# Hybrid encoder step, Mamba-2 mixer: transposes of the old-state parts in a row, decays of the first group tile by tile, and a share of the work at the mixer's end moved from VectorE to GpSimd

## The chip, the cores and the metric

One NeuronCore of one Trainium2 chip runs the whole program in one launch. The metric is the device time of one execution in microseconds (us); for before it is the median of three runs. Engines are called PE (TensorE), DVE (VectorE), ACT (ScalarE), POOL (GpSimd) and SP (SyncE, which issues the loads of the weights).

## The reference

One inference step of a two-layer trunk for 384 tokens: 256 of a new stream and 16 each of 8 running streams. Layer 0 has a Mamba-2 mixer, layer 1 latent attention; each is framed by two half-step SwiGLU blocks. The change lies in the mixer of layer 0 and where it hands over to the SwiGLU block behind it. What that mixer computes, cut from the reference:

```python
z, xbc, dt_raw = split(u @ w_in)                 # u: RMSNorm of h, 384 x 1024
xbc = silu(causal_conv(xbc, conv_buf, conv_w, conv_b))
xs, Bm, Cm = split(xbc)                          # 32 heads of 64; 4 groups with a state of 128
dt = softplus(dt_raw + dt_bias); A = -exp(A_log)
# ssd_scan, chunk by chunk:
seg    = exp(where(causal, acs_l - acs_s, -inf)) # acs = cumsum(dt * A)
y_diag = einsum(C_l . B_s * seg, xs * dt)
y_off  = einsum(C_l, state) * exp(acs)
state  = state * exp(acs[-1]) + einsum(B, xs * dt * exp(acs[-1] - acs))
y = rmsnorm((y_diag + y_off + D * xs) * silu(z), norm_g)
h = h + y @ w_out
```

Then follows `h = h + 0.5 * swiglu(rmsnorm(h, ln_ffn2[0]), ...)`, whose first products need the new h.

## The kernel before, in words

**Layout.** Activations lie transposed, features on the 128 partitions and the 384 tokens along the free axis; TT = 3 token tiles of 128: tiles 0 and 1 are the new stream, tile 2 the samples. All weights come as one stream of blocks of 128 x 1024 fp32 into four slots (`raw`). ACT copies a block into its rounded part `whi` (`hi_split`), DVE subtracts to get `wlo` (`lo_split`), and PE computes each product of 128 columns as three matmuls, xh*whi, xl*whi and xh*wlo (lines 1786 to 1788); 24 of them use up one block. A slot is free for ACT when PE has counted the block in `blk`, and for SP's next load when its `lo_split` has counted `lo_ready`.

**Order.** Nothing is scheduled automatically: each engine has its own program, written by hand, and the semaphores tie them. Around the weight stream each engine walks the same list MIX_ORDER of blocks.

**The mixer** goes over GROUPS = 4 groups g. A group has ten input blocks in_proj(g, 0..9): 0 to 3 are x, 4 and 5 are B and C, all six with a convolution (three DVE steps, L1290) and a silu on ACT; 6 to 9 are the gate z. After block 6 stand `turns(g)` (PE transposes B and x, and multiplies B and C), after 7 `first_states`, after 8 `old_state`. `y_tile(g, t)` forms the output of tile t for the eight heads of the group, in PSUM banks 0 to 3: for t >= 1 first the old-state part `yoff`, brought in by a matmul against the identity (L1979), then per head the matmul of `seg` with `xdt` (L1983), both per bank in turn. It waits for `seg`: POOL loads the cumulative sums spread over rows, ACT makes differences (`seg_diff`, eight instructions a tile, L815) and exponentials (L820), DVE multiplies by the masked C.B (`decay_cb`, L1360). `sample_states(g, 0..3)` adds to the sample streams' states (L2002; DVE's `state_add`, L1388; POOL decays them before, L556).

**y.** DVE's `y_rows` (L1395 to L1401) adds D*xs, gates with z, and splits y into `yh` (ACT) and `yl`; ACT squares it, DVE sums the squares over all groups in `sqacc` (`y_square_sum`, L1430). out_proj(g, 0..3) multiplies y with four blocks, two output columns j each; DVE adds them to `facc` (L1412, L1414). Those of group g run among group g+1's input blocks.

**The mixer's end.** For the last group y lies in `xh` and `xl` at 4 to 7. PE multiplies ones with `sqacc` for the mean square (L2056), ACT takes the root, DVE the reciprocal (L1499), and `residual(b)` scales two columns of facc (L1419) and adds them to h (L1420). `x_hi` (ACT, L695) and `x_lo` (DVE, L1174) split the new h for the SwiGLU block `gate_up(1, 2)`, whose weight blocks are gu1, gu1+1, ... PE takes gu1 column by column as x_lo delivers (L1786), then gu1+1, then the matmul of the norm's sum of squares (L1802, `norm_sum`), which DVE sums from ACT's squares (L1517, L1520).

## Time and profile before

| | |
|---|---|
| median of 3 runs | 1923.78 us (1918.68 to 1928.84) |
| profiled execution | 1929.4 us, its span 1927.6 us |
| granted PE clock, mean | 0.981 |
| PE busy | 1858.5 us (96%) |
| DVE busy | 1143.1 us (59%) |
| ACT busy | 828.4 us (43%) |
| POOL busy | 226.5 us (12%) |

The profiled execution lies 5.6 us above the median. The times of the rows are from its span's start; the mixer runs from about 290 to 655 us, its groups some 79 us each. PE busy says that an instruction was there, not at which clock; the column PEclk does. A group of rows at one line can mix shapes.

### The profile page before, as it was taken

What the parts mean: (1) busy time and instruction counts of PE and PEld (TensorE: products, weight loads), DVE (VectorE), ACT (ScalarE), POOL (GpSimd) and SP (SyncE); (2) the same over time, 40 slices, a digit from 0 to 9 for tenths busy, and PEclk for the clock granted to TensorE, in tenths of its full rate; (3) what the DMA queues carried; (4) which work ended last, traced back from release to release, by engine and by line L of the source; (5) the groups of instructions that cost most, each with busy time, mean ns of one, the idle gap of its engine ahead of it and who ended that gap; (6) DMA issues with size and microseconds to landing.
All of it is one profiled execution on the core that took longest, in us unless ns stands there. A gap on an engine that the chain in (4) does not pass through costs nothing.

```text
span 1927.6 us, 28305 instructions
## 1 busy us (share of the span) xinstructions
PE 1858.5 (96%) x10584; PEld 1758.3 (91%) x10584; DVE 1143.1 (59%) x1733; ACT 828.4 (43%) x1427; POOL 226.5 (12%) x283
## 2 busy tenths in 40 slices
PE   9999998999999899999999999998998999999997
PEld 8999998698888899999999999986777889999997
DVE  6455448587787845544674454445777745554444
ACT  5333226463564433323453333336666534333333
POOL 1000111203202000002310001113102131000110
PEclk9999999799999999999999999999999999999999
DMA  5444444354452444444444444441124533444441
GB/s 201 131 127 123 142 133 151 95 208 157 166 202 70 164 131 125 123 139 137 121 123 126 131 130 133 134 147 58 45 66 125 178 113 116 122 121 129 143 132 65
DMA packets 67652, 249.71 MB, mean 130 GB/s; under 512 B 8328, under 2 KB 9608, under 8 KB 66288
## 3 DMA queue, kind: packets, MB, share of 16 engines
q1 hardware_dynamic: 57584, 205.32, 34.8%
q0 software_dynamic: 9984, 43.24, 6.6%
q8 instruction: 56, 0.92, 0.2%
q14 instruction: 28, 0.23, 0.0%
HBM read 235.74 MB, written 12.12 MB: 129 GB/s over the span
## 4 chain that ended last, share of the span: by engine, by line
PE 85%; DVE 8%; ACT 3%; issue 1%; DMA 1%; POOL 0%; SPq 0%; DVEq 0%; ACTq 0%; POOLq 0%
PE pair L1786 23%; PE pair L1787 23%; PE pair L1788 23%; PE pair L2202 2%; PE pair L2203 1%; PE pair L2204 1%; DVE wlo L1164 1%; PE pair L1983 1%; PE pair L1793 1%; PE pair L1795 1%; PE pair L1794 1%; PE pair L2002 1%; ACT seg L815 1%; PE pair L2284 1%; PE pair L1979 1%
## 5 line engine op out<-in xcount | busy, mean ns | idle before, releaser
L1786 PE MATMUL pair<-xh,whi 128*128 128x384 f32 x1960 | 665.3, 339 | 14.8 <-DVE xl L1174 12.6
L1788 PE MATMUL pair<-xh,wlo 128*128 128x384 f32 x1960 | 658.6, 336 | 0.0
L1787 PE MATMUL pair<-xl,whi 128*128 128x384 f32 x1960 | 658.5, 336 | 0.0
L1164 DVE TENSOR_TENSOR wlo<-raw,whi 128x1024 fp32r<-128x1024 f32 (+3 forms) x372 | 463.2, 1246 | 180.5 <-ACT whi L686 171.7
L686 ACT ACTIVATE whi<-raw 128x1024 fp32r<-128x1024 f32 (+2 forms) x369 | 378.9, 1029 | 296.2 <-PE pair L1788 283.0
L1786 PEld LDWEIGHTS pair<-xh,whi 128*128 128x128 f32 x1960 | 371.1, 189 | 26.1 <-issue 15.0
L1787 PEld LDWEIGHTS pair<-xl,whi 128*128 128x128 f32 x1960 | 371.2, 189 | 1.8 <-issue 1.2
L1788 PEld LDWEIGHTS pair<-xh,wlo 128*128 128x128 f32 x1960 | 370.7, 189 | 0.0
L1184 DVE TENSOR_TENSOR tg<-pair,rstd 128x384 f32<-128x384 f32 x88 | 49.0, 557 | 332.5 <-PE pair L1788 331.8
L1786 PE MATMUL pair<-ah,whi 128*128 128x384 f32 x704 | 237.0, 337 | 3.5 <-DVE tu L1185 3.3
L1787 PE MATMUL pair<-al,whi 128*128 128x384 f32 x704 | 236.5, 336 | 0.0
L1788 PE MATMUL pair<-ah,wlo 128*128 128x384 f32 x704 | 236.5, 336 | 0.0
L705 ACT ACTIVATE tg<-tg 128x384 f32<-128x384 f32 x88 | 46.4, 527 | 350.0 <-DVE tu L1185 350.0
L1786 PEld LDWEIGHTS pair<-ah,whi 128*128 128x128 f32 x704 | 132.3, 188 | 4.7 <-DVE tu L1185 4.7
L1787 PEld LDWEIGHTS pair<-al,whi 128*128 128x128 f32 x704 | 132.4, 188 | 0.0
L1788 PEld LDWEIGHTS pair<-ah,wlo 128*128 128x128 f32 x704 | 132.3, 188 | 0.0
L527 POOL TENSOR_TENSOR sqacc<-h 128x384 f32<-128x384 f32 x6 | 5.8, 974 | 816.4 <-DVE h L1212 762.7
L695 ACT ACTIVATE xh<-h,gains 128x384 fp32r<-128x384 f32 x64 | 37.0, 612 | 119.1 <-DVE h L1212 102.6
L529 POOL TENSOR_TENSOR sqt<-h 128x384 f32<-128x384 f32 x42 | 36.6, 872 | 288.9 <-DVE h L1212 266.4
L1657 DVE TENSOR_REDUCE sqacc<-kn 128x8 f32<-128x512 f32 x64 | 43.5, 681 | 25.3 <-ACT kn L1024 25.0
L530 POOL TENSOR_TENSOR sqacc<-sqacc,sqt 128x384 f32<-128x384 f32 x42 | 58.0, 1381 | 3.3
L709 ACT ACTIVATE ah<-tu 128x384 f32 (+1 forms) x88 | 46.4, 527 | 22.6 <-DVE tu L1188 22.6
(393 smaller groups left out, 2252.5 us busy)
## 6 DMA issues: line engine op xcount, KB each, us to landing
raw<-in_stream SPq DMA_DIRECT2D x372, 512.0 KB, 3.6
S<-in_ssm POOLq DMA_DIRECT2D x4, 2048.0 KB, 8.7
out_ssm_s<-S POOLq DMA_DIRECT2D x4, 2048.0 KB, 8.0
seg<-acs_rows POOLq DMA_DIRECT2D x12, 512.0 KB, 4.9
cTb<-in_cacheT POOLq DMA_DIRECT2D x10, 512.0 KB, 4.0
kn<-rs_rows SPq DMA_DIRECT2D x16, 264.0 KB
lowC<-in_cache SPq DMA_DIRECT2D x8, 512.0 KB, 3.2
lowA<-in_cacheT POOLq DMA_DIRECT2D x6, 512.0 KB, 5.2
```

The lines of the kernel that those rows point to most:

```text
L530: step(pool.tensor_tensor(acc, acc, sqt[:, :], ALU.add))
L686: A(whi[:, r, 0:w], raw[:, r, 0:w], ACT.Copy).then_inc(hi_ready, 1)
L695: A(xh[:, k, :], h[:, k, :], ACT.Copy, scale=gains[:, m, k:k + 1]).then_inc(xh_ready, 1)
L705: A(tg[:, j, :], tg[:, j, :], ACT.Silu).then_inc(sg_ready, 1)
L709: A(ah[:, i * 2 + (n0 // 2 + j), :], tu[:, j, :], ACT.Copy).then_inc(ah_ready, 1)
L1164: V.tensor_tensor(wlo[:, r, 0:w], raw[:, r, 0:w], whi[:, r, 0:w].bitcast(F32), ALU.subtract).then_inc(lo_ready, 1)
L1184: V.tensor_tensor(tg[:, j, :], bank[2 * j][:, 0:TOK], r, ALU.mult)
L1657: V.reduce_sum(ksq[:, st, b, 8 * g:8 * g + 8], kn[:, w % 2, 0:512].rearrange("p (h d) -> p h d", h=8), axis=AX.X).then_inc(past_sum, 1)
L1786: M(out, whi[:, r, ws], mh_(k), start=first and k == k0, stop=False)
L1787: M(out, whi[:, r, ws], ml_(k), start=False, stop=False)
L1788: ins = M(out, wlo[:, r, ws], mh_(k), start=False, stop=last and k == k1 - 1)
L2202: M(bank[w % 2][:, :], ch, wkh[:, k, half], start=k == 0, stop=False)
```

## The change

It touches five things.

1. **Old-state parts.** In `y_tile`, for t >= 1, the four parts of `yoff` are brought into banks 0 to 3 by four transposes in a row, ahead of all eight heads, instead of one fp32 matmul against the identity per bank.
2. **Group 0.** ACT's silu of block 5 comes before `decay_exps`; `seg_diff` and the exponential alternate tile by tile, tiles 0 and 1 behind block 8, tile 2 behind block 9. DVE's `decay_cb(0, t)` and PE's `y_tile(0, 0)` stand where the other groups have them.
3. **Group 3.** ACT's `seg_diff(3, 2)` comes behind block 6's silu.
4. **Sums of squares** of y go from DVE to POOL in all groups, after the store of the states; DVE's gate evacuations wait for POOL's count (`sq_step`).
5. **The end.** y of group 3 has tiles of its own (`yh3`, `yl3`, in the space of `xdt` and `seg`), so all of xh and xl is free for the new h. PE's mean square comes ahead of out_proj(3, 0), and `sample_states(3, 3)` behind it. DVE evacuates two columns in one instruction (`f_add`). POOL splits the blocks gu1, gu1+1 and gu1+2, and for the last two columns scales the sum of groups 0 to 2 and adds it to h, while DVE adds the last group's part straight from PSUM. DVE takes up its own splits when POOL's last one has counted; `state_add(3, 2)` moves behind that.

PE, group 1, the second token tile, before (`pair` are the PSUM banks, L1979 the old-state part, L1983 the heads):

```order
L1979 MATMUL pair<-ident,yoff 128x128
L1983 MATMUL pair<-seg,xdt 64x128 x2
L1979 MATMUL pair<-ident,yoff 128x128
L1983 MATMUL pair<-seg,xdt 64x128 x2
L1979 MATMUL pair<-ident,yoff 128x128
L1983 MATMUL pair<-seg,xdt 64x128 x2
L1979 MATMUL pair<-ident,yoff 128x128
L1983 MATMUL pair<-seg,xdt 64x128 x2
```

and now, with the states of the first two streams and the third tile behind it (the same lines are L2007, L2011 and L2030 there):

```order
L2007 MATMUL pair<-ident,yoff 128x128 x4
L2011 MATMUL pair<-seg,xdt 64x128 x8
L2030 MATMUL pair<-xw,Bm 128x512 x2
L2007 MATMUL pair<-ident,yoff 128x128 x4
L2011 MATMUL pair<-seg,xdt 64x128 x8
```

The kinds no longer alternate within a tile; nothing else moved between them.

ACT, group 0, from the end of in_proj(0, 7) to the gates, before (whi is a block's split, seg the decays, zs the gates):

```order
L686 ACTIVATE whi<-raw 128x1024 [waits blk,raw_loaded0]
L815 ACTIVATE seg<-seg,acs 128x128 [waits seg_ld0]
L815 ACTIVATE seg<-seg,acs 128x128 x7
L815 ACTIVATE seg<-seg,acs 128x128 [waits seg_ld1,act_chain]
L815 ACTIVATE seg<-seg,acs 128x128 x7
L815 ACTIVATE seg<-seg,acs 128x128 [waits seg_ld2,act_chain]
L815 ACTIVATE seg<-seg,acs 128x128 x7
L820 ACT_TABLE_LOAD
L820 ACTIVATE seg<-seg 128x1024 [waits act_chain]
L820 ACTIVATE seg<-seg 128x1024 x2
```

and now:

```order
L721 ACTIVATE whi<-raw 128x1024 [waits blk,raw_loaded0]
L850 ACTIVATE seg<-seg,acs 128x128 [waits seg_ld0]
L850 ACTIVATE seg<-seg,acs 128x128 x7
L854 ACTIVATE seg<-seg 128x1024 [waits act_chain]
L850 ACTIVATE seg<-seg,acs 128x128 [waits seg_ld1]
L850 ACTIVATE seg<-seg,acs 128x128 x7
L854 ACTIVATE seg<-seg 128x1024 [waits act_chain]
L721 ACTIVATE whi<-raw 128x1024 [waits blk,raw_loaded1]
L850 ACTIVATE seg<-seg,acs 128x128 [waits seg_ld2]
L850 ACTIVATE seg<-seg,acs 128x128 x7
L854 ACTIVATE seg<-seg 128x1024 [waits act_chain]
```

Each tile's exponential follows its differences, and no table load stands between them.

DVE at the mixer's end, from the last two residuals to the norm's sums, now (L1455 is f_add, L1471 and L1472 the residual, L1220 x_lo, L1210 a split, L1432 state_add, L1544 and L1547 the sums of squares):

```order
L1455 TENSOR_TENSOR facc<-facc,pair 128x768 [waits blk]
L1471 TENSOR_TENSOR facc<-facc,rstd 128x768 [waits f_evac]
L1472 TENSOR_TENSOR h<-h,facc 128x768 [waits dve_chain]
L1220 SCALAR_TENSOR_TENSOR xl<-h,gains,xh 128x384 [waits xh_ready] x2
L1471 TENSOR_TENSOR facc<-pair,rstd 128x768 [waits h_part,blk]
L1472 TENSOR_TENSOR h<-h,facc 128x768 [waits dve_chain]
L1220 SCALAR_TENSOR_TENSOR xl<-h,gains,xh 128x384 [waits xh_ready] x2
L1210 TENSOR_TENSOR wlo<-raw,whi 128x1024 [waits hi_ready,lo_ready]
L1432 TENSOR_TENSOR S<-S,pair 128x512 [waits s_dec,state_ps]
L1432 TENSOR_TENSOR S<-S,pair 128x512 [waits s_dec]
L1544 TENSOR_TENSOR sqacc<-facc 128x384 [waits sq_step]
L1547 TENSOR_TENSOR sqacc<-sqacc,facc 128x384 [waits sq_step,dve_chain] x6
```

and beside it POOL, which had nothing there before but the store:

```order
L554 TENSOR_TENSOR sqacc<-sqacc,zs 128x384 [waits y_sq]
L554 TENSOR_TENSOR sqacc<-sqacc,zs 128x384 [waits y_sq,sq_step] x3
L561 TENSOR_TENSOR wlo<-raw,whi 128x1024 [waits lo_ready,hi_ready,sq_step]
L591 TENSOR_TENSOR facc<-facc,rstd 128x768 [waits f_evac,y_rstd]
L594 TENSOR_TENSOR h<-h,facc 128x768 [waits h_part]
L561 TENSOR_TENSOR wlo<-raw,whi 128x1024 [waits lo_ready,hi_ready] x2
L598 DMA out_ssm_s<-S 128x4096 [waits state_ready]
```

Three splits, a scaling and an add left DVE's row for POOL's, and DVE's split of gu1+3 waits for `lo_ready`.

The diff, cut to its core:

```diff
@@ tiles
+            with ExitStack() as rows_first:
+                xdt = sb("xdt", [P, TT, 512], F32, rows_first)
+                seg = sb("seg", [P, TT, 1024], F32, rows_first)
+            yh3 = sb("yh3", [P, 4, TOK], F32R, ssd)
+            yl3 = sb("yl3", [P, 8, TOK], F32R, ssd)
@@ helpers
         def y_hi(g, k):
-            return yh[:, k, :] if g < GROUPS - 1 else xh[:, 4 + k, :]
+            return (yh if g < GROUPS - 1 else yh3)[:, k, :]
+        def y_summed(g):
+            return 3 * KD - 2 + 4 * (g + 1)
@@ GpSimd
+            def y_square_sum(g):
+                for i in range(4):
+                    pool.wait_ge(y_sq, 4 * g + i + 1)
+                    if g or i > 1:
+                        step(pool.tensor_tensor(sqacc[:, 0, :], sqacc[:, 0, :], zs[:, i, :], ALU.add))
+                    elif i == 1:
+                        step(pool.tensor_tensor(sqacc[:, 0, :], zs[:, 0, :], zs[:, 1, :], ALU.add))
+
+            def lo_split(n):
+                pool.wait_ge(hi_ready, n + 1)
+                pool.wait_ge(lo_ready, n)
+                pool.tensor_tensor(wlo[:, n % SLOTS, :], raw[:, n % SLOTS, :], whi[:, n % SLOTS, :].bitcast(F32),
+                                   ALU.subtract).then_inc(lo_ready, 1)
...
+                if g == GROUPS - 1:
+                    y_square_sum(g)
+                    lo_split(BASE["gu1"])
+                    pool.wait_ge(y_rstd, 1)
+                    pool.wait_ge(f_evac, 8 * g)
+                    pool.tensor_tensor(facc[:, 6:8, :], facc[:, 6:8, :], bc(rstd[:, 0, :], (P, 2, TOK), 1),
+                                       ALU.mult).then_inc(h_part, 1)
+                    pool.wait_ge(h_part, 1)
+                    pool.tensor_tensor(h[:, 6:8, :], h[:, 6:8, :], facc[:, 6:8, :], ALU.add).then_inc(h_part, 1)
+                    lo_split(BASE["gu1"] + 1)
+                    lo_split(BASE["gu1"] + 2)
                 pool.wait_ge(state_ready, 8 * g + 8)
                 pool.dma_start(T["ssm_s"][g], S[:, :, :]).then_inc(s_store, 16)
                 if g < GROUPS - 1:
+                    y_square_sum(g)
                     pool.wait_ge(s_store, 16 * (g + 1))
                     pool.dma_start(S[:, :, :], T["ssm"][g + 1]).then_inc(s_ld, 16)
@@ ScalarE
                 in_proj(g, 5)
                 if g == 0:
+                    silu(0, 5)
                     decay_exps()
-                else:
+                elif not last:
                     seg_diff(g, 2)
...
                 in_proj(g, 6)
+                if last:
+                    seg_diff(g, 2)
...
                 in_proj(g, 8)
                 if g == 0:
-                    for t in range(TT):
+                    for t in range(2):
                         seg_diff(g, t)
-                    seg_exps(g)
+                        seg_exp(g, t)
                 in_proj(g, 9)
+                if g == 0:
+                    seg_diff(g, 2)
+                    seg_exp(g, 2)
...
+            hi_split(n + 3)
+            for b in range(3):
+                x_hi(2, 2 * b)
+                x_hi(2, 2 * b + 1)
+                hi_split(n + 4 + b)
+            for k in range(4):
+                x_square(k)
+            x_hi(2, 6)
+            x_hi(2, 7)
             for k in range(4, KD):
                 x_square(k)
@@ VectorE
                     if g:
-                        dve.wait_ge(y_sq, 4 * g)
+                        dve.wait_ge(sq_step, y_summed(g - 1))
...
             def residual(b):
                 two = slice(2 * b, 2 * b + 2)
-                dve.wait_ge(f_evac, 8 * (GROUPS - 1) + 2 * b + 2)
-                step(V.tensor_tensor(facc[:, two, :], facc[:, two, :], bc(rstd[:, 0, :], (P, 2, TOK), 1), ALU.mult))
+                if b < 3:
+                    f_add(GROUPS - 1, b)
+                    dve.wait_ge(f_evac, 8 * (GROUPS - 1) + 2 * b + 2)
+                    src = facc[:, two, :]
+                else:
+                    dve.wait_ge(blk, CRED + out_block(GROUPS - 1, b) + 1)
+                    dve.wait_ge(h_part, 2)
+                    src = f_pair(GROUPS - 1, b)
+                step(V.tensor_tensor(facc[:, two, :], src, bc(rstd[:, 0, :], (P, 2, TOK), 1), ALU.mult))
                 V.tensor_tensor(h[:, two, :], h[:, two, :], facc[:, two, :], ALU.add).then_inc(h_new, 2)
...
+            n = out_block(GROUPS - 1, 0)
+            f_add(GROUPS - 2, 2)
+            lo_split(n + 1)
+            f_add(GROUPS - 2, 3)
+            lo_split(n + 2)
             dve.wait_ge(y_std, 1)
-            step(V.reciprocal(rstd[:, 0, :], std[:, :]))
+            V.reciprocal(rstd[:, 0, :], std[:, :]).then_inc(y_rstd, 1)
+            lo_split(n + 3)
+            dve.wait_ge(y_rstd, 1)
+            for b in range(4):
+                residual(b)
+                x_lo(2, 2 * b)
+                x_lo(2, 2 * b + 1)
...
+            dve.wait_ge(lo_ready, BASE["gu1"] + 3)
             gate_up(1, 2, norm_square_sum)
@@ TensorE
+                if t:
+                    for i in range(4):
+                        nc.tensor.transpose(bank[i][:, tiles(t)], yoff[:, t - 1, tiles(i)], ident[:, :])
                 for i in range(4):
-                    if t:
-                        M(bank[i][:, tiles(t)], yoff[:, t - 1, tiles(i)], ident[:, :], start=True, stop=False,
-                          skip_group_check=True)
...
             out_proj(GROUPS - 2, 3)
+            pe.wait_ge(sq_step, y_summed(GROUPS - 1))
+            M(bank[5][:, 0:TOK], ones[:, :], sqacc[:, 0, :], start=True, stop=True).then_inc(y_sum_ps, 1)
             out_proj(GROUPS - 1, 0)
-            pe.wait_ge(state_ready, 8 * GROUPS - 2)
-            pe.wait_ge(y_sq, 4 * GROUPS + 1)
-            M(bank[4][:, 0:TOK], ones[:, :], sqacc[:, 0, :], start=True, stop=True).then_inc(y_sum_ps, 1)
+            pe.wait_ge(y_std, 1)
+            sample_states(GROUPS - 1, 3)
```

## Rows read from the trace of the kernel before

**Rows 1.** Page: busy time and share of the span; then the chain's shares.
```profile
PE 1858.5 (96%) x10584; PEld 1758.3 (91%) x10584; DVE 1143.1 (59%) x1733; ACT 828.4 (43%) x1427; POOL 226.5 (12%) x283
...
PE 85%; DVE 8%; ACT 3%; issue 1%; DMA 1%; POOL 0%; SPq 0%; DVEq 0%; ACTq 0%; POOLq 0%
```

**Rows 2.** Windows: stretch, its us, busy us per engine, PEclk, DMA share, GB/s.
```profile
358.11:377.90 19.79, 19.79 (x82) 12.03 (x83) 6.39 (x9) 1.12 (x3) 2.66 (x3) 0.50 0.31 105
440.80:458.80 18.00, 18.00 (x121) 13.74 (x120) 13.20 (x18) 4.79 (x8) 7.24 (x7) 1.00 0.53 162
573.90:578.70 4.80, 0.15 (x1) 0.00 (x0) 3.32 (x6) 4.75 (x16) 0.00 (x0) 0.73 0.40 109
578.70:583.00 4.30, 4.26 (x21) 4.26 (x21) 3.56 (x7) 4.29 (x5) 0.00 (x0) 0.51 0.40 122
```

**Rows 3.** PE timeline: start, us, line, operation, count, [idle before, its releaser].
```profile
334.26 1.49 PE L1945 MATMUL pair<-BC 128*128 128x128 f32 x6
...
358.11 1.98 PE L1983 MATMUL pair<-seg,xdt 128*64 128x128 f32 x16 [3.13 <-DVE seg L1360]
...
380.73 1.13 PE L2002 MATMUL pair<-xw,Bm 32*128 32x512 f32 x4
...
440.83 1.09 PE L1983 MATMUL pair<-seg,xdt 128*64 128x128 f32 x16
446.16 0.38 PE L1979 MATMUL pair<-ident,yoff 128*128 128x128 f32 x2
...
449.20 1.13 PE L2002 MATMUL pair<-xw,Bm 32*128 32x512 f32 x4
...
458.85 1.13 PE L2002 MATMUL pair<-xw,Bm 32*128 32x512 f32 x4
...
505.44 1.47 PE L1949 MATMUL pair<-ident,xsT 128*128 128x128 f32 x12
...
578.74 0.90 PE L1937 MATMUL pair<-ident,BC 128*128 128x128 f32 x3 [4.69 <-ACT BC L771]
...
610.03 1.14 PE L2002 MATMUL pair<-xw,Bm 32*128 32x512 f32 x8
...
655.37 0.91 PE L1802 MATMUL pair<-sqacc,ones 128*128 128x384 f32 x2 [0.45 <-DVE sqacc L1520]
```

**Rows 4.** ACT timeline, group 0: differences, then exponentials of the decays.
```profile
343.04 7.41 ACT L815 ACTIVATE seg<-seg,acs 128x128 f32<-128x128 f32 x24
...
351.76 2.96 ACT L820 ACTIVATE seg<-seg 128x1024 f32<-128x1024 f32 x3
```

**Rows 5.** DVE timeline, group 0 and the mixer's end.
```profile
350.44 1.64 DVE L1164 TENSOR_TENSOR wlo<-raw,whi 128x1024 fp32r<-128x1024 f32 x1
...
356.84 3.49 DVE L1360 TENSOR_TENSOR seg<-seg,Gm 128x1024 f32<-128x1024 f32 x3
...
626.62 2.54 DVE L1499 RECIPROCAL rstd<-std 128x384 f32<-128x384 f32 x1
629.20 0.96 DVE L1419 TENSOR_TENSOR facc<-facc,rstd 128x768 f32<-128x768 f32 x1
...
632.28 1.01 DVE L1414 TENSOR_TENSOR facc<-facc,pair 128x384 f32<-128x384 f32 x2
...
651.79 3.52 DVE L1520 TENSOR_TENSOR sqacc<-sqacc,facc 128x384 f32<-128x384 f32 x6
```

**Rows 6.** Groups by line: count, busy us, mean ns, idle before; last a DMA issue.
```profile
L1164 DVE TENSOR_TENSOR wlo<-raw,whi 128x1024 fp32r<-128x1024 f32 (+3 forms) x372 | 463.2, 1246 | 180.5 <-ACT whi L686 171.7
...
L530 POOL TENSOR_TENSOR sqacc<-sqacc,sqt 128x384 f32<-128x384 f32 x42 | 58.0, 1381 | 3.3
L556 POOL TENSOR_TENSOR S<-S,dec 128x512 f32<-128x512 f32 x32 | 41.0, 1310 | 101.2 <-PE pair L1960 101.2
...
L568 POOL DMA_DIRECT2D S<-in_ssm x3 | 1.7, 557 | 23.2 <-DMA out_ssm_s<-S 23.2
...
seg<-acs_rows POOLq DMA_DIRECT2D x12, 512.0 KB, 4.9
```

More of the change, by code:

```diff
@@ L787, in in_proj @@
                       ACT.Copy).then_inc(cout_ready, 1)
[L788 removed]
+                if 1 <= b <= 6 and (g or b < 6):
                     silu(g, b - 1)
@@ L1485, in _ @@
                 if g == 0:
-                    for t in range(TT):
-                        decay_cb(g, t)
+                    decay_cb(g, 2)
                 state_add(g, 0)
```

143 lines of the change are left out of this document (49 added, 94 removed).

## The prediction

> **What bounds the kernel now.** I read the page first: TensorE (PE) is busy 96% of the span and holds 85% of the chain that ended last; VectorE (DVE) holds 8%, ScalarE (ACT) 3% [rows 1]. So a change of order pays only where PE waits, where its clock is low, or where its own work gets shorter. Next I read the windows of granted clock inside the mixer, 260 to 655 us. In group 0 there is a stretch of 19.8 us in which PE is busy throughout at a granted clock of 0.50, 1.2 instead of 2.4 GHz; it follows a wait. The same tiles of group 1 run at 1.00. In group 3 a wait of 4.7 us, with ACT busy through it, is followed by 4.3 us at 0.51 [rows 2]. The PE timeline then gives the waits and the price of each step [rows 3], and those of ACT, DVE and the POOL rows what the moved work costs [rows 4 to 6]. The reader should see in them that DVE, not PE, carries the mixer's end: from the last y matmul (610.03) to the norm matmul (655.37) are 45.3 us, and the norm matmul waits for DVE's sums.
>
> **The old-state parts.** In y_tile(g, 1) and (g, 2) PE now alternates a two-pass fp32 matmul (0.38 us) and a pair of 64-wide ones; a tile takes 449.20 - 446.16 = 3.04 us. Afterwards four transposes stand in a row, then eight heads. Twelve transposes in a row took 1.47 us, less the tail 0.11 each, so four take 0.44; eight heads in a row (16 passes) start 440.83 and cost about 1.02 before the next block [rows 3]. That is 1.46, so 1.6 us less per tile. There are two such tiles per group. PE is the bound there in groups 1 and 2, and DVE's y_rows waits for the last tile in group 3, so all six tiles of groups 1 to 3 count: **-9.5 us**. The two of group 0 give another 3.2 at full clock.
>
> **Group 0.** The wait is 3.13 us, ended by DVE's decay product L1360 [rows 3]. DVE has three such products in 3.49 us, behind evacuation 9 in its order [rows 5], and ACT first does all 24 differences (7.41 us) and then three exponentials (2.96) [rows 4]. After the change ACT does 8 differences (2.47) and one exponential (0.99). It starts when in_proj(0, 7) ends, near 341.5, and the exp table is still loaded, since silu no longer comes between. The first exponential ends near 345, DVE's product near 346.5. PE wants it after old_state(0), near 349. So this wait goes, with 2.5 us to spare. What is late next is tile 2: its product stands behind evacuation 9 and costs PE about 0.4. The clock: from the first tile to the end of in_proj(1, 0) group 0 takes 380.73 - 358.11 = 22.6 us; group 1 takes 458.85 - 440.83 = 18.0 for the same and one in_proj more (4.3 us, from the end of its first tile, 441.85, to 446.16), 13.7. The low clock costs 8.9 [rows 3]. A second edit: ACT's silu of block 5 no longer waits behind the decay exponentials and a table load, so the B transposes start at once; but the products of B and C still wait for those exponentials (they read its PSUM banks), and these begin 2.2 us later than before. I put the products at 333.0 instead of 334.26: 1.3 gained. The seg loads start 2.2 us later too, near 335.5; with 4.9 us to landing [rows 6] the first is there long before ACT's difference at 341.5, and the next have 3 and 7 us more. Sum: 3.1 + 8.9 + 3.2 + 1.3 - 0.4 = **-16.1 us**.
>
> **Sums of squares of groups 0 to 2.** DVE loses up to four adds of 384 per group. POOL gets them at 1.38 each [rows 6], 5.5 us. They stand there behind the store of the old states and ahead of the load of the next ones, and POOL already idles there for that store's landing, 23.2 us in three groups, 7.7 each [rows 6]: the adds fit in. Even if they didn't, that load runs in a stretch where PE needs the states only at the next first_states, some 30 us on. Evacuations 6 to 9 now wait for POOL's sum, done some 25 us earlier. I count nothing in groups 1 and 2. Two columns in one instruction free a PSUM bank 0.5 us later, about what the lighter DVE gives back.
>
> **Group 3.** PE waits 4.69 us for silu of B and C on ACT [rows 3], and ACT is busy for 4.75 of these 4.80 us [rows 2]. One difference tile, 2.47 us [rows 4], now stands behind that silu; of what DVE saves with its four adds (3.52 us for six such adds [rows 5], so some 2.4 for four) only about 0.3 arrives, because ACT is full. So 2.7 of 4.69 go and 2.0 stay. At 0.51 the 4.3 us behind it cost about 2.1. Whether the clock still falls after a wait of 2 us, the rows leave open, and I keep that cost: **-2.7**.
>
> **The mixer's end**, from the last y matmul as 0. y_rows on DVE is unchanged, 7.0 us. Then come two f_adds with two splits between; the second f_add waits for PE (out_proj(2, 3) ends at 9.4) and the reciprocal (2.54) ends at 14.5, where before it ended at 19.1. Before it PE needs POOL's four adds, 4.5 to 10.2, and waits for them some 0.9; PE has slack here. After one more split (15.6) come the residuals: f_add 1.0, product 0.96, add 0.96, ACT's hop 0.7, two x_lo about 1.1 (as two f_adds of 384, 1.01) [rows 5], with semaphores 4.8 us each, the last without its f_add 3.8: 33.8 if nothing disturbs them. But POOL works from 20.7: a split, a product and an add of 768, two splits. An add of 384 takes 1.38 and a product of 512 takes 1.31 us [rows 6]; by length the split of 1024 lies between 2.6 and 3.7. I take 3.6 and 2.8 for 768, since both inputs are whole tiles as in the 384 add; together 16.4, to 37.6 with the hops. h_part arrives at 30.2, before residual(3) wants it at 32. Next to POOL a DVE split took 1.64 instead of 1.25 us [rows 5, 6]; I add a third to DVE's SBUF-only work, 1.0 per residual, three times: 36.9. ACT then has the last squares and the split of gu1+3, to 38.5; DVE's own split 1.2, a state_add 1.25 that came later before, and seven sums 4.1 (3.52 for six) [rows 5]: the norm matmul at 45.1 against 45.3. **About 0.** The three splits and two partial steps that leave DVE are given back by the wait for POOL's last split, the slower shared stretch and the state_add moved ahead of the sums.
>
> The Trainium skill (GPSIMD Engine Reference, Performance versus the Vector engine) measures tensor_tensor on GpSimd at 4497 ns for 2048 fp32 and about 2.6 cycles per element. That would make a split some 2.5 us, an estimate from that page; the end would stay, since DVE sets it.
>
> **Sum.** 9.5 + 16.1 + 2.7 + 0 = 28.3 us; I round the hand-made hops up to 28.8. The profiled execution took 1929.4 (span 1927.6) and would take 1900.6. It lies 5.6 above the median of the three runs, 1923.8, so the forecast for the median is **1895 us**, 1.5% faster.
>
> **Rivals.**
> - *DVE and POOL exclude each other at the end.* For it: the 1.64 us split. Against it: a full exclusion by POOL's 1.3 us products would give 2 us and more. Its price: POOL's 16.4 us and DVE's SBUF-only 9 us in a row from 20.4 end at 45.8 instead of 36.9, so 9 us are lost: 1904. The Trainium skill (SBUF — State Buffer, Who interferes with whom) states it so: a DVE instruction with two SBUF inputs and a GpSimd instruction that reads SBUF use one pair, whoever comes first keeps it for its whole instruction. The rows show a third more, not that. 10%.
> - *The clock in group 0 stays low* because the tiles are light work, not because of the wait. Against it: group 1's tiles run at 1.00 [rows 2]. Price: 8.9 less what shorter tiles save, about 7: 1902. 7%.
> - *Transposes in a row don't cost 0.11* ahead of 64-wide matmuls (0.42 each, 1.2 us per tile, eight tiles): 10 us lost, 1905. 5%.
> - *The end gains too* (no disturbance, clock kept in group 3): 2 to 8 us more, 1887 to 1893; the main case reaches down to 1889. 12%.
> - *Slower:* POOL's splits starve PE. gu1, gu1+1 and gu1+2 can't be multiplied before POOL has split them, and DVE itself waits for the last. Five POOL operations stand in that chain; the gain of 28.8 is eaten when they take 45 instead of 16.4 us, 9 us each. The price at 11 us each is 38 us: 1933. For it: nothing in the trace shows a 1024-long POOL operation. Against it: by length 3.7 at most, and twice that loses 16 of 28.8. 2%.
> - *The change only swaps waits*, within 0.5%: group 0's first product is late again because seg lands late (its exponential would have to be 7 us later). Then 3.1 and 8.9 us stay lost and 16.8 are gained, 1907; with the end 9 us worse as well, 1916. 4%, the half of it within 0.5%.
>
> **Chances and range.** Main case 1895 (1889 to 1901): 60%. The rivals as given. The 8-in-10 range takes in the lock, the clock and the transposes: 1885 to 1905. A measurement of this kernel tells about 0.5% (9.6 us) from no change; only the last two cases and a part of the bad ends together reach above 1914: faster 0.94, same 0.04, slower 0.02.
>
> **What would show it.** No PE wait on the decay product before the first y tile and a clock near 1.00 from there on; y tiles 1 and 2 in 1.5 us; PE's wait in turns(3) near 2 us; POOL's splits near 3.6 us with no PE wait on them; DVE split and residual products a third longer beside them; the norm matmul 45 us behind the last y matmul. Wrong at once: a y tile still at 3 us, a clock of 0.50 in group 0, or a POOL split over 5 us.

## The result, and the profile after

Against the kernel before the change, run beside it, the ratio is 0.9905, 95% interval 0.9888 to 0.9923: medians 1907.42 us (six runs, 1901.71 to 1909.52) and 1924.02 (six runs, 1918.68 to 1928.84). It is faster by 0.95%, and the forecast of 1895 (1885 to 1905) was too good by 12 us. The profiled execution took 1907.38 us, span 1905.6, where the one of before took 1929.4, span 1927.6. The page after, busy times and the shares of the chain that ended last, against [rows 1]:

```profile
PE 1838.9 (97%) x10552; PEld 1747.1 (92%) x10552; DVE 1142.5 (60%) x1698; ACT 825.9 (43%) x1425; POOL 260.6 (14%) x303
...
PE 83%; DVE 9%; ACT 3%; issue 2%; DMA 1%; POOL 0%; SPq 0%; DVEq 0%; ACTq 0%; POOLq 0%
```

DVE's busy time hardly moved although work left it, and its share of the chain rose. The windows after (the columns of [rows 2]) are PE's products of B and C in group 0, the y tiles of group 0 with what stands between them, the like stretch of group 1, and the 4.7 us behind PE's wait in turns(3):

```profile
332.00:337.00 5.00, 4.49 (x20) 4.52 (x21) 3.59 (x7) 2.25 (x5) 2.75 (x4) 0.50 0.30 66
...
350.48:365.92 15.44, 15.04 (x114) 12.32 (x113) 12.95 (x18) 8.05 (x17) 6.98 (x7) 1.00 0.62 188
426.81:441.91 15.10, 15.10 (x115) 12.45 (x116) 13.33 (x18) 4.76 (x8) 7.22 (x7) 1.00 0.64 191
556.30:561.00 4.70, 4.67 (x25) 4.67 (x26) 4.45 (x9) 4.67 (x11) 0.00 (x0) 0.64 0.47 149
```

The tiles of group 0 ran at 0.50 in [rows 2] and run at 1.00 now; a short stretch ahead of them is at 0.50. PE's timeline after, the rows that answer to [rows 3]:

```profile
332.51 1.62 PE L1973 MATMUL pair<-BC 128*128 128x128 f32 x6 [2.03 <-ACT dec L844]
...
350.48 1.09 PE L2011 MATMUL pair<-seg,xdt 128*64 128x128 f32 x16
...
358.88 0.66 PE L2007 MATMUL pair<-ident,yoff 128*128 128x128 f32 x4 [0.40 <-DVE seg L1404]
...
365.92 1.13 PE L2030 MATMUL pair<-xw,Bm 32*128 32x512 f32 x4
...
381.47 0.41 PE L1814 MATMUL pair<-yh,whi 128*128 128x384 f32 x1 [0.44 <-DVE facc L1453]
...
426.81 1.09 PE L2011 MATMUL pair<-seg,xdt 128*64 128x128 f32 x16
...
434.75 0.66 PE L2007 MATMUL pair<-ident,yoff 128*128 128x128 f32 x4
435.34 1.09 PE L2011 MATMUL pair<-seg,xdt 128*64 128x128 f32 x16
436.36 1.13 PE L2030 MATMUL pair<-xw,Bm 32*128 32x512 f32 x4
...
556.33 0.55 PE L1965 MATMUL pair<-ident,BC 128*128 128x128 f32 x3 [2.08 <-ACT BC L806]
...
584.18 1.13 PE L2030 MATMUL pair<-xw,Bm 32*128 32x512 f32 x4
...
633.88 0.91 PE L1830 MATMUL pair<-sqacc,ones 128*128 128x384 f32 x2 [1.81 <-DVE sqacc L1547]
```

Read against [rows 3]: the first y tile starts 7.6 us earlier and waits for nothing; the end of group 0's tiles (365.92 against 380.73) has gained 14.8 us, the last y matmul (584.18 against 610.03) 25.85. Then the gain shrinks: from there to the norm matmul it took 45.3 us and takes 49.7. Behind the norm matmul both kernels take the same, 1272.2 and 1271.7. So of the terms that the forecast added up, the mixer's end missed most. There DVE's timeline shows

```profile
590.09 1.90 DVE L1445 SCALAR_TENSOR_TENSOR yl<-zs,ang,yh 128x384 fp32r<-128x384 f32 x2
...
592.78 1.49 DVE L1210 TENSOR_TENSOR wlo<-raw,whi 128x1024 fp32r<-128x1024 f32 x1
...
606.76 2.09 DVE L1471 TENSOR_TENSOR facc<-facc,rstd 128x768 f32<-128x768 f32 x1
608.96 2.44 DVE L1472 TENSOR_TENSOR h<-h,facc 128x768 f32<-128x768 f32 x1
612.09 1.98 DVE L1220 SCALAR_TENSOR_TENSOR xl<-h,gains,xh 128x384 fp32r<-128x384 f32 x2 [0.69 <-ACT xh L730]
613.99 0.94 DVE L1455 TENSOR_TENSOR facc<-facc,pair 128x768 f32<-128x768 f32 x1
614.96 2.15 DVE L1471 TENSOR_TENSOR facc<-facc,rstd 128x768 f32<-128x768 f32 x1
617.21 0.96 DVE L1472 TENSOR_TENSOR h<-h,facc 128x768 f32<-128x768 f32 x1
...
620.97 2.55 DVE L1472 TENSOR_TENSOR h<-h,facc 128x768 f32<-128x768 f32 x1
...
627.38 1.22 DVE L1210 TENSOR_TENSOR wlo<-raw,whi 128x1024 fp32r<-128x1024 f32 x1 [2.03 <-ACT whi L721]
```

and POOL's, the same stretch:

```profile
588.73 2.31 POOL L554 TENSOR_TENSOR sqacc<-sqacc,zs 128x384 f32<-128x384 f32 x2 [10.88 <-ACT zs L866]
592.16 2.96 POOL L554 TENSOR_TENSOR sqacc<-sqacc,zs 128x384 f32<-128x384 f32 x2 [1.12 <-ACT zs L866]
605.63 2.41 POOL L561 TENSOR_TENSOR wlo<-raw,whi 128x1024 fp32r<-128x1024 f32 x1 [10.51 <-ACT whi L721]
608.00 2.59 POOL L591 TENSOR_TENSOR facc<-facc,rstd 128x768 f32<-128x768 f32 x1
610.67 2.45 POOL L594 TENSOR_TENSOR h<-h,facc 128x768 f32<-128x768 f32 x1
613.59 2.71 POOL L561 TENSOR_TENSOR wlo<-raw,whi 128x1024 fp32r<-128x1024 f32 x1 [0.47 <-ACT whi L721]
620.36 2.36 POOL L561 TENSOR_TENSOR wlo<-raw,whi 128x1024 fp32r<-128x1024 f32 x1 [4.06 <-ACT whi L721]
```

Lay the two over each other. POOL's split ends at 605.63 + 2.41 = 608.04, DVE's product at 606.76 + 2.09 = 608.85, 0.81 later. POOL's product ends at 610.59, DVE's add at 611.40, 0.81 later; 616.30 and 617.11; 622.72 and 623.52. Four times DVE's instruction ends 0.80 to 0.81 us behind POOL's, however early it began: it stood still until POOL had done, and only then did its work. (It ends 0.81 behind and not 0.96, the length of its row alone; no row explains the 0.15.) The x_lo pair at 612.09 stands still as well, until POOL's add ends at 613.12. It works the other way round too: POOL's product begins at 608.00, while DVE's still runs, and its add at 610.67, while DVE's add does, so POOL's 2.59 and 2.45 hold up to 0.85 and 0.73 us of standing still. The f_add at 613.99, one of whose inputs is PSUM, runs beside a POOL split in its usual 0.94. Against 0.96 and 1.15 alone, the five stretched rows lose 1.13 + 1.48 + 0.83 + 1.19 + 1.59 = 6.2 us. Beside POOL's four adds of the squares, at 588.73 to 595.12, DVE's rows are stretched too: y_rows ends 7.7 us after its start, at 591.99, where before it took 6.9, and the split at 592.78 takes 1.49 instead of 1.22. These adds stay on POOL in all the experiments on the end below.

### The profile page after: what moved, and what is told of

The parts are those of the page before. It is cut to its first block, busy times and chain, and to the rows that moved or that the text cites. A ratio compares the mean times of both kernels' runs of the same rounds, so it can differ in the third digit from the quotient of the medians.

```text
span 1905.6 us, 28242 instructions
## 1 busy us (share of the span) xinstructions
PE 1838.9 (97%) x10552; PEld 1747.1 (92%) x10552; DVE 1142.5 (60%) x1698; ACT 825.9 (43%) x1425; POOL 260.6 (14%) x303
## 4 chain that ended last, share of the span: by engine, by line
PE 83%; DVE 9%; ACT 3%; issue 2%; DMA 1%; POOL 0%; SPq 0%; DVEq 0%; ACTq 0%; POOLq 0%
PE pair L1814 23%; PE pair L1816 23%; PE pair L1815 23%; PE pair L2227 2%; PE pair L2228 1%; PE pair L2229 1%; DVE cy L1336 1%; DVE wlo L1210 1%; DMA lowA<-in_cacheT 1%; PE pair L1821 1%; PE pair L1823 1%; PE pair L1822 1%; PE pair L2309 1%; ACT seg L850 1%; PE pair L2011 1%
## 5 line engine op out<-in xcount | busy, mean ns | idle before, releaser
L1814 PE MATMUL pair<-xh,whi 128*128 128x384 f32 x1928 | 652.4, 338 | 16.0 <-DVE xl L1220 13.6
L1816 PE MATMUL pair<-xh,wlo 128*128 128x384 f32 x1928 | 646.7, 335 | 0.0
L1815 PE MATMUL pair<-xl,whi 128*128 128x384 f32 x1928 | 646.5, 335 | 0.0
L1210 DVE TENSOR_TENSOR wlo<-raw,whi 128x1024 fp32r<-128x1024 f32 (+2 forms) x369 | 461.3, 1252 | 185.1 <-ACT whi L721 176.3
L1814 PEld LDWEIGHTS pair<-xh,whi 128*128 128x128 f32 x1928 | 363.9, 189 | 26.1 <-issue 14.4
L1815 PEld LDWEIGHTS pair<-xl,whi 128*128 128x128 f32 x1928 | 363.9, 189 | 1.5 <-issue 1.0
L1816 PEld LDWEIGHTS pair<-xh,wlo 128*128 128x128 f32 x1928 | 363.7, 189 | 0.0
L1685 DVE TENSOR_REDUCE sqacc<-kn 128x8 f32<-128x512 f32 x64 | 43.5, 681 | 25.7 <-ACT kn L1070 25.5
L1220 DVE SCALAR_TENSOR_TENSOR xl<-h,gains,xh 128x384 fp32r<-128x384 f32 x64 | 41.9, 686 | 25.5 <-ACT xh L730 25.4
```

The costliest lines, as they stand in the source:

```text
L1210: V.tensor_tensor(wlo[:, r, 0:w], raw[:, r, 0:w], whi[:, r, 0:w].bitcast(F32), ALU.subtract).then_inc(lo_ready, 1)
L1220: V.scalar_tensor_tensor(out=xl[:, k, :], in0=h[:, k, :], scalar=gains[:, m, k:k + 1], in1=xh[:, k, :].bitcast(F32), op0=ALU.mult, op1=ALU ...
L1685: V.reduce_sum(ksq[:, st, b, 8 * g:8 * g + 8], kn[:, w % 2, 0:512].rearrange("p (h d) -> p h d", h=8), axis=AX.X).then_inc(past_sum, 1)
L1814: M(out, whi[:, r, ws], mh_(k), start=first and k == k0, stop=False)
L1815: M(out, whi[:, r, ws], ml_(k), start=False, stop=False)
L1816: ins = M(out, wlo[:, r, ws], mh_(k), start=False, stop=last and k == k1 - 1)
```

## The experiments

In the table, "y end" is the start of the row behind the last y matmul, "norm" the norm matmul, both from PE's timeline, and the way between them.

| kernel | y end | norm | way | median us | ratio to before |
|---|---|---|---|---|---|
| before | 610.03 | 655.37 | 45.3 | 1924.0 to 1927.9, five medians | 1 |
| after | 584.18 | 633.88 | 49.7 | 1907.4 | 0.9905 (0.9888 to 0.9923) |
| e1_rows | 591.97 | 637.30 | 45.3 | 1911.0 | 0.9924 (0.9903 to 0.9946) |
| e2_group0 | 597.45 | 642.77 | 45.3 | 1913.7 | 0.9947 (0.9926 to 0.9968) |
| e3_end_only | 609.09 | 658.81 | 49.7 | 1933.8 | 1.0042 (1.0024 to 1.0059) |
| e4_pool_left_out | 581.72 | 625.20 | 43.5 | 1901.8 | 0.9885 (0.9864 to 0.9906) |
| e5_splits_on_dve | 583.96 | 629.35 | 45.4 | 1903.9 | 0.9873 (0.9850 to 0.9897) |
| e6_part_on_dve | 581.85 | 630.83 | 49.0 | 1904.6 | 0.9884 (0.9860 to 0.9908) |
| e7_all_on_dve | 580.95 | 626.06 | 45.1 | 1899.6 | 0.9862 (0.9837 to 0.9888) |
| e8_woven | 584.69 | 628.16 | 43.5 | 1899.1 | 0.9847 (0.9826 to 0.9869) |
| e9_one_input | 581.92 | 625.99 | 44.1 | one run | |
| e10_split_beside_reciprocal | 579.93 | 623.44 | 43.5 | 1899.1 | 0.9866 (0.9844 to 0.9888) |
| e11_single_columns | 581.89 | 623.83 | 41.9 | 1899.0 | 0.9855 (0.9830 to 0.9880) |
| e12_before_again | 611.01 | 656.34 | 45.3 | 1928.2 | 1.0013 (0.9995 to 1.0032) |

**The parts apart.** e1 is the kernel before with the transposes in a row and nothing else:

```
+                if t:
+                    for i in range(4):
+                        nc.tensor.transpose(bank[i][:, tiles(t)], yoff[:, t - 1, tiles(i)], ident[:, :])
                 for i in range(4):
-                    if t:
-                        M(bank[i][:, tiles(t)], yoff[:, t - 1, tiles(i)], ident[:, :], start=True, stop=False,
-                          skip_group_check=True)
```

> Kernel before, with the old-state parts transposed in a row and nothing else. If a transpose ahead of the 64-wide matmuls costs 0.11 us, as the trace of the changed kernel says (a tile in 1.56 instead of 3.04 us), six tiles give 9 us at full clock and the two of group 0, which still run at 1.2 GHz here, about 2.5 us each: a span 13 to 14 us below before. If part of that is lost again because VectorE becomes the bound behind the tiles, less than 9.

Measured: 18.1 us at the y end, where 13 to 14 were expected. Groups 1 to 3, from the first y tile of group 1 to the y end, took 610.03 - 440.83 = 169.2 and take 159.7: 9.5. The rest is group 0, and PE's timeline of e1 shows why:

```profile
359.51 1.83 PE L1983 MATMUL pair<-seg,xdt 128*64 128x128 f32 x16 [3.13 <-DVE seg L1360]
361.28 1.12 PE L1979 MATMUL pair<-ident,yoff 128*128 128x128 f32 x4
...
364.77 0.66 PE L1979 MATMUL pair<-ident,yoff 128*128 128x128 f32 x4
```

The wait of 3.13 us is as before, and the clock falls as before, but four transposes take 1.12 us in tile 1 and 0.66 in tile 2, 3.5 us later: the low stretch ends within tile 1, where [rows 2] has it last 19.8 us. The three traces with the alternating tiles and that wait (before, e3, e12) all have the long one. Five of e1's six runs lie within 1 us of the traced one (1910.7 to 1911.5), so its trace shows e1's usual case; still it is one trace. As far as it goes, either part, the row of transposes or the earlier decays, wins back most of the low clock, and the two gains can't be added.

e2 is the kernel before with the new order of group 0 alone (silu of block 5 first, differences and exponentials tile by tile, products and y_tile(0, 0) where the other groups have them):

```
+                    silu(0, 5)
                     decay_exps()
...
-                    for t in range(TT):
+                    for t in range(2):
                         seg_diff(g, t)
-                    seg_exps(g)
+                        seg_exp(g, t)
```

> Kernel before, with the order of group 0 alone (silu of block 5 first, decays tile by tile, first y tile ahead of block 9). The forecast had 12.9 us here without the two tiles (3.1 the wait, 8.9 the clock, 1.3 the products of B and C, less 0.4). The trace of the changed kernel says 11.7, because the low clock behind turns(0) now reaches into in_proj(0, 7). Rival: the clock stays at 1.2 GHz in the light tiles when these still alternate, then 4 us or less.

It gains 440.83 - 428.62 = 12.2 us to the first y tile of group 1 and 12.6 at the y end. The window from 350.20 to 366.00, with the alternating tiles in it, ran at 1.00. That rules out the prediction's rival by which the clock is low because the tiles are light work: without the wait the same tiles keep it. e1's 18.1 and e2's 12.6 would make 30.7; the changed kernel has 25.85, with group 3's part as well. The difference is, as far as rows show it, the clock counted twice.

e3 is the changed kernel with the transposes, group 0 and group 3 as before, so that the sums of squares and the new end are left:

```
-                if t:
-                    for i in range(4):
-                        nc.tensor.transpose(bank[i][:, tiles(t)], yoff[:, t - 1, tiles(i)], ident[:, :])
...
-                    silu(0, 5)
...
-                    seg_diff(g, 2)
```

> Changed kernel with the first three parts undone: alternating old-state parts, the old order of group 0 and of group 3's last differences. What is left is the end with GpSimd's share, the sums of squares on GpSimd and the paired evacuations. The forecast had about 0 for this. If the end is worse by the 4.4 us that the traces show between the last y matmul and the norm matmul, the time is 2 to 4 us above before (the lighter VectorE gives 1 to 2 back in group 3); at 0 or below, the loss lies elsewhere.

The end, with the sums on POOL and the paired evacuations, makes the kernel slower, by 0.42% (0.24 to 0.59), and its way is 49.7 us, the same as after. The spans differ by 4.4, which is the way; the medians by 7.4, where 2 to 4 were expected. For the other 3 us no row was found.

**Is it POOL?** e4 is the changed kernel without POOL's five steps at the end. No other engine does them, so three low parts, and in two columns of h the share of groups 0 to 2, are missing:

```
-                    lo_split(BASE["gu1"])
...
-                    pool.tensor_tensor(h[:, 6:8, :], h[:, 6:8, :], facc[:, 6:8, :], ALU.add).then_inc(h_part, 1)
+                        pool.wait_ge(hi_ready, n + 1)
+                        pool.wait_ge(lo_ready, n)
+                        pool.sem_inc(lo_ready, 1)
```

> Changed kernel in which GpSimd only counts its five steps at the end and does not do them: the splits of gu1, gu1+1 and gu1+2 and the two steps on columns 6 and 7 are left out, so the result lacks them. Theory (VectorE's instructions with two SBUF inputs stand still while GpSimd reads): seven of them took 7 us more than alone, so the norm matmul comes 6 to 7 us sooner, 43 instead of 49.7 us behind the last y matmul, and the span is 6 to 7 us shorter than the changed kernel's. Rival (the new order of splits, states and sums and the wait for ScalarE's split of gu1+3 cost it): at most 1 to 2 us shorter.

The way is 43.5, 6.2 less, and the stretched rows had lost 6.2. Every product and add of 768 is back at 0.96. So the new order of the end is worth 45.3 - 43.5 = 1.8 us if POOL's steps cost nothing, and DVE standing still for them takes 6.2.

e5, e6 and e7 give the steps back to DVE, in parts and together. The three splits go behind the adds of the residuals:

```
             for b in range(4):
                 residual(b)
+                if b:
+                    lo_split(n + 3 + b)
                 x_lo(2, 2 * b)
```

and residual(3) is done like the others:

```
-                if b < 3:
-                    f_add(GROUPS - 1, b)
...
-                    dve.wait_ge(h_part, 2)
-                    src = f_pair(GROUPS - 1, b)
+                f_add(GROUPS - 1, b)
```

> The changed kernel with its three splits of gu1 to gu1+2 back on VectorE, each between the add of a residual and its x_lo pair; GpSimd keeps the sums of squares and the product and add of residual(3). The way from the last y matmul to the norm matmul took 45.3 us before, 49.7 after and 43.4 with none of the five steps. Theory (each of the two engines stands still for the other's whole instruction): in the changed kernel the five steps stretch five VectorE instructions by 1.13, 1.48, 0.83, 1.19 and 1.59 us, 6.2 in all; here two steps are left, with some 2.5 of it, and the splits add 1.2 each less the 0.7 of the hop to ScalarE that each now fills: 43.4 + 2.5 + 1.5 = 47.4 us, 2.3 us under the changed kernel. Rival (the order of the end costs the time, not the other engine): VectorE gets 3.6 us of work more and wins nothing, 50 us or more.

> The changed kernel with residual(3) wholly on VectorE; GpSimd keeps the sums and the three splits. Theory: three stretched instructions, some 3.7 us, and on VectorE one f_add of 0.95 more, since product and add stood there already: 43.4 + 3.7 + 0.95 = 48.0 us from the last y matmul to the norm matmul, 1.7 under the changed kernel. Rival (order): VectorE has 0.95 more to do and the way is 50.6.

> The changed kernel with all five steps back on VectorE; GpSimd only sums the squares. Theory: no VectorE instruction is stretched; 43.4 + 0.95 + 1.5 = 45.9 us from the last y matmul to the norm matmul, 3.8 under the changed kernel, and a split and a product at 1.2 and 0.96 us throughout. Rival (order): 43.4 with less work, so at least 43.4 + 0.95 + 3.6 = 48, and with what the order costs the 49.7 of the changed kernel.

e7 has 45.1 where 45.9 was expected and the rival had 48 or more: with all five steps on DVE, three splits of 1.22 and an f_add of 0.95 more work, the way is 4.6 us shorter than after. e6, with POOL's three splits, has 49.0 (48.0 expected): in its DVE timeline the products next to them take 2.09, 2.68 and 2.63 us, 4.5 lost. e5 has 45.4 (47.4 expected): its two POOL steps cost 0.43 and 1.46 us, and DVE's splits cost less than I had put, since each fills the 0.7 us hop to ScalarE. The theory holds for all three; which steps are on POOL decides, not the order.

**Whose inputs matter?** e9 keeps POOL busy at the same places with steps that read less:

```
-                pool.tensor_tensor(wlo[:, n % SLOTS, :], raw[:, n % SLOTS, :], whi[:, n % SLOTS, :].bitcast(F32),
-                                   ALU.subtract).then_inc(lo_ready, 1)
+                pool.tensor_copy(wlo[:, n % SLOTS, :], raw[:, n % SLOTS, :]).then_inc(lo_ready, 1)
...
+                    pool.memset(facc[:, 6:8, :], 0.0).then_inc(h_part, 1)
...
+                    pool.memset(h[:, 6:8, :], 0.0).then_inc(h_part, 1)
```

> The changed kernel, but GpSimd's five steps at the mixer's end read less: the three splits are copies of raw (one SBUF input), the product and the add are constant fills (no input). It leaves out the low parts of three weight blocks and a quarter of the residual, so only the traces of the two engines are read. Theory (VectorE stands still only while a GpSimd instruction with two SBUF inputs runs, or one that reads SBUF at all): beside the fills no VectorE instruction is stretched, a product of 768 takes 0.96 us and an x_lo pair 1.15; beside the copies it decides which of the two it is. Rival (any GpSimd access to SBUF holds VectorE up, writes too): VectorE's products and adds beside the fills are stretched as in the changed kernel, to 2.0 us and more.

POOL's timeline of e9, and DVE's:

```profile
604.36 0.73 POOL L590 MEMSET facc<- 128x768 f32 x1
605.15 0.74 POOL L592 MEMSET h<- 128x768 f32 x1
608.69 1.04 POOL L561 CAST wlo<-raw 128x1024 fp32r<-128x1024 f32 x1 [2.80 <-ACT whi L719]
613.78 1.05 POOL L561 CAST wlo<-raw 128x1024 fp32r<-128x1024 f32 x1 [4.05 <-ACT whi L719]
```

```profile
604.50 0.96 DVE L1469 TENSOR_TENSOR facc<-facc,rstd 128x768 f32<-128x768 f32 x1
605.56 0.96 DVE L1470 TENSOR_TENSOR h<-h,facc 128x768 f32<-128x768 f32 x1
...
609.25 1.29 DVE L1469 TENSOR_TENSOR facc<-facc,rstd 128x768 f32<-128x768 f32 x1
...
614.41 1.22 DVE L1470 TENSOR_TENSOR h<-h,facc 128x768 f32<-128x768 f32 x1
```

Beside the two fills, which only write, DVE's product and add run in 0.96. Beside the copies, which read one tile, they are stretched, and end at 610.54 and 615.63, again 0.81 and 0.80 us behind POOL's 609.73 and 614.83. So both kinds of POOL read tried here, of two tiles and of one, hold up a DVE instruction with two SBUF inputs, and POOL's fills don't. The Trainium skill (SBUF — State Buffer, Who interferes with whom) states just that, with the pair kept for the whole instruction and DVE instructions of at most one SBUF input free of it; the runs agree in each point: the common 0.81 us behind POOL's end, and the f_add in its usual 0.94.

**A better end.** e8 is e7 with hops filled and the sums earlier:

```
             for b in range(3):
+                hi_split(n + 4 + b)
                 x_hi(2, 2 * b)
                 x_hi(2, 2 * b + 1)
-                hi_split(n + 4 + b)
...
-                if b:
-                    lo_split(n + 3 + b)
+                if b < 3:
+                    lo_split(n + 4 + b)
+                else:
+                    state_add(GROUPS - 1, 2)
```

> As the one before, with the order of the end woven anew: ScalarE splits a block high before each x_hi pair and the fourth gate_up block ahead of the last pair, VectorE has a split (behind the last residual the state_add) between every residual and its x_lo pair, and the norm's sums come ahead of the split of gu1+3. Theory: VectorE's work is the bound once it stands still for nobody; what fills its hops comes off: 43 to 43.5 us from the last y matmul to the norm matmul, some 6 us under the changed kernel, near 1900. Rival (PE is what paces the end): no gain against the kernel without weaving, 45.9.

43.5 us as expected, and 1899.1: faster than both kernels, with an interval wholly below that of the changed one. PE no longer waits for the sums. Against e7 the total gains nothing that can be told; e7's trace had reached the y end 3.7 us earlier.

e10 tests the same rule from the side where it allows something: one split on POOL, beside the reciprocal.

```
-            lo_split(n + 3)
+            dve.wait_ge(lo_ready, n + 4)
...
                     y_square_sum(g)
+                    lo_split(out_block(g, 3))
```

> The woven kernel, with one split given to GpSimd again, that of out_proj(3, 3), which falls beside VectorE's reciprocal (one SBUF input, 2.55 us). Theory (only VectorE instructions with two SBUF inputs stand still): the split runs 2.4 us beside the reciprocal and the f_add, the reciprocal stays at 2.55, and VectorE's way is up to 1.2 us shorter, less what is left of the split when the first product of the residuals wants to start: 42.5 to 43.2 us from the last y matmul to the norm matmul against 43.4. Rival (any two instructions exclude each other): the reciprocal stretches to 4 us or more and the way is 44.5 or more. The total moves by less than a measurement tells.

DVE's timeline of e10, then POOL's:

```profile
592.40 2.55 DVE L1523 RECIPROCAL rstd<-std 128x384 f32<-128x384 f32 x1 [0.39 <-ACT std L926]
596.14 0.95 DVE L1450 TENSOR_TENSOR facc<-facc,pair 128x768 f32<-128x768 f32 x1 [1.18 <-PE pair L1809]
```

```profile
593.45 2.40 POOL L561 TENSOR_TENSOR wlo<-raw,whi 128x1024 fp32r<-128x1024 f32 x1 [2.57 <-ACT whi L713]
```

The reciprocal, with its one SBUF input, takes its 2.55 us beside the split, and the split its 2.40, so the rule holds. The way stays 43.5: what DVE saves it waits for PE, 1.18 us in front of the first f_add.

e11 gives groups 0 to 2 their single-column evacuations back:

```
+                if g < GROUPS - 1:
+                    for x in range(2):
+                        j, src = 2 * b + x, f_pair(g, b)[:, x, :]
...
+                            V.tensor_tensor(facc[:, j, :], facc[:, j, :], src, ALU.add).then_inc(f_evac, 1)
```

> As the one before, and the f_adds of groups 0 to 2 free their PSUM columns one by one again instead of in pairs. In the changed kernel TensorE waits five times 0.44 us for such a pair in groups 1 to 3 (before: 0.36 and 0.95). Theory: those waits go or shrink, and from the first y tile of group 0 to the first of group 3 it takes about 1 us less than the changed kernel's 222.95 us. Rival (the pairs cost nothing, TensorE waits for VectorE's other work): as long as in the changed kernel. It would be the fastest of all, 1897 to 1899.

The five waits of 0.44 us are gone, and from the first y tile of group 0 to that of group 2 it takes 500.81 - 350.18 = 150.6 us against 152.2 after and in e7: 1.6 us. To group 3 the gain is 2.0 (221.0 against 222.95), and in the total it doesn't show.

**The spread.** e12 is the kernel before, unchanged.

> The kernel before, once more, for a second trace. Its runs lie in two groups, near 1921 and near 1929, with mean granted clocks of 0.985 to 0.987 and 0.980 to 0.981; the trace shown is of the upper group. Theory (the clock after a wait of TensorE comes back sooner in some runs): if this trace is of the lower group, every row agrees with the first trace but for one or two stretches behind a wait, where the granted clock is 0.50 in the one and near 1.00 in the other, and these hold the 5 to 8 us. Rival (the runs differ everywhere a little, by the DMAs): the distance to the first trace grows evenly. If it falls in the upper group, it agrees with the first trace within 1 us at the last y matmul (610.03) and tells nothing.

Its traced run (1930.5) fell in the upper group, agrees with the first trace within 1 us at the y end, and tells nothing of the lower one. What separates the two groups of before, 5 to 8 us, stays open. That a clock can differ at the same place is shown elsewhere. Behind PE's wait in turns(3), windows of after (above, 0.64) and of e4:

```profile
555.50:560.20 4.70, 4.69 (x35) 4.70 (x36) 4.60 (x9) 4.67 (x11) 0.00 (x0) 1.00 0.46 139
```

The waits are 2.08 and 2.06 us, the work is the same, and from there to the first y tile the changed kernel takes 573.43 - 556.33 = 17.1 us and e4 570.97 - 555.51 = 15.5. The changed kernel, e5, e8 and e11 have the long form, e4, e6, e7, e9 and e10 the short. At the end, behind a wait of 3.65 us for x_lo (e11, first) and of 3.66 (e10, second):

```profile
618.50:623.80 5.30, 5.30 (x30) 5.25 (x31) 5.09 (x9) 2.31 (x4) 0.00 (x0) 1.00 0.00 0
```

```profile
616.50:623.40 6.90, 6.86 (x30) 6.80 (x31) 6.66 (x11) 2.36 (x4) 0.00 (x0) 0.75 0.03 5
```

The same two blocks of matmuls take 5.3 us or 6.9; e8 has the long form too. That is the whole difference between e11's way and e10's, not an edit's doing.

## Why the prediction was wrong, step by step

- **Old-state parts, 9.5 us in groups 1 to 3: right, the last 0.4 by luck.** In e1 it is 9.5. Group 1's two tiles took 3.04 and 3.15 us (446.16 to 449.20, 450.26 to 453.41) and take 1.55 and 1.61 after (432.14 to 433.69, 434.75 to 436.36), which makes 3.03 per group and 9.1 in three groups. The other 0.4 is clock: from the wait in turns(3) to group 3's first y tile, before takes 17.5 us and e1 17.1.
- **Group 0, 16.1: 14.0.** The wait went, the clock held, tile 2 waits 0.40 for its product, all as forecast. The B and C products' 1.3 came to 0.25: they did start earlier (332.51), but behind that very wait of 2.03 the clock is 0.50 now (the window at 332), and first_states starts at 341.57 against 341.82. The step took an earlier start for a gain without asking what the clock does behind the wait that is left. How long it stays low differs from trace to trace of the same order: from these products to first_states it takes 9.1 us after and in e2, 6.2 in e4, e7, e9 and e10. Paired evacuations, which I had set at nothing, cost two waits of 0.44 before group 1's tiles where before had one of 0.36.
- **The share of the clock.** The 8.9 us that I gave to the vanished wait aren't that wait's alone: with transposes in a row the low stretch ended after some 3 us even with the wait (e1, one trace). That the sum still held is luck: the two were in one change. Added up from e1 and e2 it would have been at least 4.9 too high.
- **Group 3, 2.7: right.** The wait fell from 4.69 to 2.08. The low clock behind it stayed in some executions and not in others; I kept it at full price.
- **The end, "about 0": +4.4, the step that failed.** The overlap was wrong: DVE's instructions beside POOL were to run on, a third longer, 3 us in all. They stood still, and the five rows lost 6.2. The other 1.1 us is a start of the residuals 0.5 later and a wait of 0.55 for PE. In front of that later start stand the stretched y_rows, which I had "unchanged, 7.0 us", and the stretched split, and POOL's last add of squares, which was held up by DVE in turn. POOL was faster than sized (2.41 and 2.59 us against 3.6 and 2.8), which shortened the rows that stood still; by my sizes, an estimate, the loss would have been the rival's 9. That rival, exclusion, had 10%.
- **Why it had so little.** My evidence against it was one DVE split of 1.64 us instead of 1.25 beside POOL's products of the states: "a full exclusion ... would give 2 us and more". That is a wrong inference. Under exclusion the stretch is what is left of POOL's instruction when DVE's begins, and anything from nothing to its whole length can be left; a single row of 0.4 extra excludes nothing. What tells them apart is the end of both rows, DVE's minus POOL's, the same each time. The trace of before had it. Beside that split POOL's two products take 3.02 us together, while the shortest such product takes 1.03: the first ends at 351.00 and the split 1.08 later, at 352.08; the second stood still for the split, took 2.0 and ended 0.9 behind it. Here is one more, from DVE's timeline of before and then POOL's, ahead of the mixer, where POOL sums `sqacc`; the last row holds the two products:

```profile
233.80 1.71 DVE L1164 TENSOR_TENSOR wlo<-raw,whi 128x1024 fp32r<-128x1024 f32 x1 [0.24 <-ACT whi L686]
```

```profile
233.22 1.21 POOL L530 TENSOR_TENSOR sqacc<-sqacc,sqt 128x384 f32<-128x384 f32 x1
...
349.97 3.02 POOL L556 TENSOR_TENSOR S<-S,dec 128x512 f32<-128x512 f32 x2
```

The split ends at 235.51 and POOL's add at 234.43: 1.08 again, though this one is stretched by 0.49 and the other by 0.42. So the right answer stood in the trace that the forecast was made from.
- **POOL's speed.** The estimate from the Trainium skill (GPSIMD Engine Reference, Performance versus the Vector engine), 2.5 us for a split, was nearer than mine by length, though by its 4497 ns for twice the elements it would be 2.25: measured are 2.36 to 2.41, and 2.71 once, for the split that began at 613.59 while x_lo still ran. My own sizes came from means (1.31 for a product of 512) that already held standing still: alone it takes 1.03. "The end would stay, since DVE sets it" doesn't hold: where DVE stands still for POOL, POOL's speed sets how long.
- **From the profiled time to the median, 5.6.** I carried the offset of before (profile above median) to the changed kernel. Its profiled run lies on its own median (1907.38 and 1907.42). Of the 12.4 us missed, 6.8 are terms (28.8 less 22.0 by the spans), 5.6 this offset: a run above its median says where that run lay, not where the next kernel's will. The three runs of before also lay low: later medians of it are 1925.8 to 1927.9. Neither miss alone leaves the range: without the 4.4 of the end, or without the 5.6, the time would have been inside 1885 to 1905.

## What to carry to other kernels

Before work goes from VectorE to GpSimd, look at what VectorE runs at that time: beside instructions with PSUM or one SBUF input the help is free (a reciprocal, an f_add), beside instructions with two SBUF inputs it costs VectorE the rest of every GpSimd instruction that reads SBUF. To see whether two engines exclude each other, subtract the ends of their rows and not their lengths. Here 12.5 us of GpSimd rows, meant to relieve VectorE of some 4.6 us, took 6.2 from it, and the same kernel with that work back on VectorE is the faster (1899 us). A wait before a stretch of light TensorE work is worth more than its own length, but its clock must be priced once for all edits that touch the stretch.
